# A last phase of two joined transformer blocks: the last norm and the gates move behind the join, three sums share one inverse root, the square of the polynomial goes to ScalarE

## What is computed

```python
attn = rms_norm(attn, attn_out_g) * silu(g_attn)          # 512 wide
ssm = gelu(y)                                             # 512 wide
ssm = ssm * sigmoid(ssm @ w_glu + b_glu)
ssm = rms_norm(ssm, ssm_out_g) * silu(g_ssm)
mixed = concatenate([attn, ssm]) @ w_out                  # 1024 x 1024
x = x + rms_norm(mixed, post_norm_g)
```

## Time and profile before

| | |
|---|---|
| median of 3 runs | 5829.93 us (5826.6 to 5834.68) |
| profiled execution, time | 5826.38 us |
| profiled execution, span | 5824.6 us |
| last phase, from SP's first load at 5492.85 us to the end | 332 us |
| PE busy in the whole span | 5316.9 us (91%) |
| DVE busy in the whole span | 3248.5 us (56%) |
| ACT busy in the whole span | 2129.4 us (37%) |
| mean granted clock of the tensor engine | 0.962 |

### The profile page before, as it was taken

One profiled execution on the slowest core, in us unless ns is written; L12 is line 12 of the kernel. 1 busy time (PEld: TensorE's weight loads), 2 busy tenths in 40 slices (PEclk: granted clock), 3 DMA queues, 4 the chain that ended last, 5 costly groups with the idle time before them and its releaser, 6 DMA issues. The chain is left out here.

```text
span 5824.6 us, 77622 instructions
## 1 busy us (share of the span) xinstructions
PE 5316.9 (91%) x24587; PEld 3508.7 (60%) x24922; DVE 3248.5 (56%) x6128; ACT 2129.4 (37%) x3190; POOL 707.8 (12%) x901
## 2 busy tenths in 40 slices
PE   6999999499999999999999999599995599999688
PEld 3555555366666666666666666355554477777365
DVE  3433433477676767777777777433335544443277
ACT  3111111144443545555555554222222433333243
POOL 0000000100000000000000000001003399100000
PEclk9999999699999999999999999799997799999899
DMA  3111211356464647777777676422322300000433
GB/s 136 57 50 54 72 50 50 115 176 192 159 207 150 211 152 238 237 237 240 239 232 234 229 227 204 161 93 103 103 89 97 82 5 8 6 6 6 170 108 101
DMA packets 424599, 769.80 MB, mean 132 GB/s; under 512 B 57440, under 2 KB 142368, under 8 KB 422816
## 3 DMA queue, kind: packets, MB, share of 16 engines
q1 hardware_dynamic: 363984, 607.16, 31.5%
q10 hardware_dynamic: 33216, 87.05, 4.9%
q0 software_dynamic: 27280, 74.02, 4.0%
HBM read 628.36 MB, written 139.76 MB: 132 GB/s over the span
## 5 line engine op out<-in xcount | busy, mean ns | idle before, releaser
L1070 DVE TENSOR_TENSOR w_lo<-stage,w_hi 128x1024 bf16<-128x1024 f32 (+1 forms) x800 | 929.6, 1178 | 201.3 <-ACT w_hi L939 142.3
L939 ACT ACTIVATE w_hi<-stage 128x1024 fp32r<-128x1024 f32 (+1 forms) x800 | 791.7, 1017 | 575.9 <-PE GU L773 291.2
L770 PE MATMUL GU<-w_hi,x_hl 128*128 128x512 f32 x2048 | 860.1, 420 | 19.0 <-DVE x_hl L1075 7.6
L771 PE MATMUL GU<-w_hi,x_hl 128*128 128x512 f32 x2048 | 811.6, 396 | 0.0
L636 PE MATMUL PJ<-w_in_sb,xT 128*128 128x512 f32 x1280 | 579.6, 607 | 41.9 <-ACT w_in_sb L376 31.5
L773 PE MATMUL GU<-w_lo,x_bf 128*128 128x512 bf16 x1920 | 480.6, 381 | 7.7
L770 PEld LDWEIGHTS GU<-w_hi,x_hl 128*128 128x128 f32 x2048 | 386.5, 189 | 135.1 <-issue 27.9
L770 PE MATMUL Y<-w_hi,a_hl 128*128 128x512 f32 x1024 | 456.8, 446 | 0.0
L636 PEld LDWEIGHTS PJ<-w_in_sb,xT 128*128 128x128 f32 x1280 | 244.2, 195 | 332.8 <-issue 286.2
L771 PEld LDWEIGHTS GU<-w_hi,x_hl 128*128 128x128 f32 x2048 | 387.5, 189 | 82.9
L771 PE MATMUL Y<-w_hi,a_hl 128*128 128x512 f32 x1024 | 404.4, 395 | 0.0
(11 more groups left out here) (537 smaller groups left out, 8752.2 us busy)
## 6 DMA issues: line engine op xcount, KB each, us to landing
stage<-in_expert_w_gate_up_dram SPq DMA_DIRECT2D x512, 512.0 KB, 5.2
stage<-in_expert_w_down_dram SPq DMA_DIRECT2D x224, 512.0 KB, 6.7
expert_rows<-zero_y SPq DMA_DIRECT2D x16, 2048.0 KB, 10.0
b_gu<-in_expert_b_gate_up_dram ACTq DMA_DIRECT2D x128, 256.0 KB, 4.9
expert_rows<-acted ACTq DMA_DIRECT2D x64, 512.0 KB, 2.9
b_d<-in_expert_b_down_dram ACTq DMA_DIRECT2D x32, 512.0 KB, 8.0
stage<-in_expert_w_down_dram SPq DMA_DIRECT2D x64, 256.0 KB, 3.3
z<-z_sb SPq DMA_DIRECT2D x16, 992.0 KB, 8.1
```

Of the source, the lines that this page charges most:

```text
L770: pe.matmul(out, high(k), w_high(k), start=(k == first), stop=False)
L771: pe.matmul(out, low(k), w_high(k), start=False, stop=False)
L939: act.activation(w_hi[:, c, ks, :], staged, ACT.Copy).then_inc(s["hi_done"], 1)
L1070: dve.tensor_tensor(w_lo[:, c, ks, :], staged, w_hi[:, c, ks, :], ALU.subtract).then_inc(s["lo_done"], 1)
```

## The change

- VectorE's order in body(t) becomes: g_lo(t), c_lo(t-1), pre(t), polynomial (t+1), ssm(t), gelu(t+1), join(t), `o_n` and `out` of t-2 (`add_x`), at t = 0 the low parts of the second weight, silu(t+1).
- The sum of squares of OUT goes into a third column of `ss`, and `join` makes the inverse root of tile t-2's sum in the same chain as its own two. Before the chain it also waits for `sumsq_o`. The last two tiles keep a chain of their own.
- ScalarE makes y squared (`square_y`) for t+1 ahead of tanh_p(t), after a wait for the loads of t+1. VectorE's polynomial is one operation, (y_sq + 1/GELU_A) * y, and the tanh's scale takes the factor GELU_A.
- `join` no longer waits for `silu_ready`.
- SP's and the tensor engine's instructions stay as they are.

```diff
         @block.scalar
         def _(act):
+            def square_y(t, par):
+                act.wait_ge(s["in_loaded"], t * per_in + per_in)
+                act.activation(y_sq[:, :], y_in[:, par, :], ACT.Square).then_inc(s["y_sq_ready"], 1)
+
             def ahead(t, par):
 
                 act.wait_ge(s["poly_ready"], t + 1)
-                act.activation(tanh_y[:, :], poly[:, :], ACT.Tanh, scale=GELU_S).then_inc(s["tanh_y_ready"], 1)
-                act.wait_ge(s["in_loaded"], t * per_in + per_in)
+                act.activation(tanh_y[:, :], poly[:, :], ACT.Tanh, scale=GELU_S * GELU_A).then_inc(s["tanh_y_ready"], 1)
...
+                if has_next:
+                    square_y(t + 1, 1 - par)
                 if has_this:
                     act.wait_ge(s["pre_ready"], t + 1)
                     act.activation(tanh_p[:, :], pre[:, :], ACT.Tanh, scale=0.5).then_inc(s["tanh_p_ready"], 1)
...
                 if has_prev:
                     act.wait_ge(s["o_ps"], t)
-                    if is_step(t, TILES):
-                        act.wait_ge(s["out_ready"], t - 1)
-                    act.activation(sq_o[:, :], OUT[1 - par][:, :], ACT.Square, accum_out=ss_o[:, :]).then_inc(s["sumsq_o"], 1)
-
+                    act.activation(sq_o[:, :], OUT[1 - par][:, :], ACT.Square, accum_out=ss[:, 1 - par, 2:3]).then_inc(s["sumsq_o"], 1)
+
+            square_y(0, 0)
             ahead(0, 0)
...
                 dve.wait_ge(s["in_loaded"], t * per_in + per_in)
-                y = y_in[:, par, :]
-                ch.link(dve.tensor_tensor(poly[:, :], y, y, ALU.mult))
-                ch.link(dve.tensor_scalar(poly[:, :], poly[:, :], GELU_A, 1.0, ALU.mult, ALU.add))
-                dve.tensor_tensor(poly[:, :], poly[:, :], y, ALU.mult).then_inc(s["poly_ready"], 1)
+                dve.wait_ge(s["y_sq_ready"], t + 1)
+                dve.scalar_tensor_tensor(poly[:, :], y_sq[:, :], 1.0 / GELU_A, y_in[:, par, :],
+                                         ALU.add, ALU.mult).then_inc(s["poly_ready"], 1)
...
-            def join(t, par, has_prev):
-
+            def join(t, par, has_prev, has_two):
+
+
+                n = 3 if has_two else 2
                 dve.wait_ge(s["sumsq"], t + 1)
                 dve.tensor_scalar(ss[:, par, 0:1], ss[:, par, 0:1], 1.0 / ATTN_W, EPS, ALU.mult, ALU.add)
+                if has_two:
+                    dve.wait_ge(s["sumsq_o"], t - 1)
+                    dve.tensor_scalar(ss[:, par, 2:3], ss[:, par, 2:3], 1.0 / D, EPS, ALU.mult, ALU.add)
                 ch.link(dve.tensor_scalar(ss[:, par, 1:2], ss[:, par, 1:2], 1.0 / (16 * SSM_W), EPS, ALU.mult, ALU.add))
-                rsqrt(dve, ch, rstd[:, :], ss[:, par, :], nt[:, :])
-                dve.wait_ge(s["silu_ready"], t + 1)
+                rsqrt(dve, ch, rstd[:, 0:n], ss[:, par, 0:n], nt[:, 0:n])
...
-            def last_norm(t, par, reused):
-                dve.wait_ge(s["sumsq_o"], t + 1)
-                inv_rms(dve, ch, rstd_o[:, :], ss_o[:, :], nt_o[:, :], D, EPS)
-                ch.link(dve.scalar_tensor_tensor(o_n[:, :], OUT[par][:, :], rstd_o[:, :], gain_post[:, :], ALU.mult, ALU.mult))
+            def add_x(t, par, reused):
+                ch.link(dve.scalar_tensor_tensor(o_n[:, :], OUT[par][:, :], rstd[:, 2:3], gain_post[:, :], ALU.mult, ALU.mult))
...
                 if has_prev:
                     low_cat(t - 1)
-                if has_two:
-                    last_norm(t - 2, par, reused)
                 bias(t)
-                if is_step(t, 0):
-                    low_weights()
                 if has_next:
                     gelu_in(t + 1, 1 - par)
                 unit(t)
                 if has_next:
                     gelu_out(t + 1, 1 - par)
+                join(t, par, has_prev, has_two)
+                if has_two:
+                    add_x(t - 2, par, reused)
+                if is_step(t, 0):
+                    low_weights()
+                if has_next:
                     gates(t + 1, 1 - par)
-                join(t, par, has_prev)
```

More of the change, by code:

```diff
@@ L2653, in output_phase @@
         x2 = sb("x2_6", [P, 2, D])
+        y_sq = sb("y_sq", [P, SSM_W])
         poly = sb("poly", [P, SSM_W])
@@ L2664, in output_phase @@
                             (("sq_a", ATTN_W), ("sq_s", SSM_W), ("sq_o", D)))
[L2665 to L2668, removed]
+        ss = sb("ss6", [P, 2, 3])
+        rstd = sb("rstd6", [P, 3])
+        nt = sb("nt6", [P, 3])
         cat = sb("cat", [P, 2, SSM_W])
@@ L2677, in output_phase @@
         OUT = [pb("OUT0", 2 * BANK), pb("OUT1", 2 * BANK)]
-        names = """gains glu_in out_in ident_ready w_high w_low in_loaded x_loaded poly_ready tanh_y_ready gelu_ready gT_ps g_hi_ready gT_sb gl_ps
+        names = """gains glu_in out_in ident_ready w_high w_low in_loaded x_loaded y_sq_ready poly_ready tanh_y_ready gelu_ready gT_ps g_hi_ready gT_sb gl_ps
             pre_ready tanh_p_ready ssm_ready sumsq sumsq_a tanh_g_ready silu_ready cat_ready cT_ps c_hi_ready cT_sb o_ps sumsq_o out_ready
@@ L2871, in last_norm @@
                 dve.tensor_tensor(out[:, par, :], o_n[:, :], x2[:, par, :], ALU.add).then_inc(s["out_ready"], 1)
+            def last_norm(t, par):
+                dve.wait_ge(s["sumsq_o"], t + 1)
+                inv_rms(dve, ch, rstd[:, 2:3], ss[:, par, 2:3], nt[:, 2:3], D, EPS)
+                add_x(t, par, True)
             def low_weights():
@@ L2917, in _ @@
             low_cat(TILES - 1)
-            last_norm(TILES - 2, 0, True)
-            last_norm(TILES - 1, 1, True)
+            last_norm(TILES - 2, 0)
+            last_norm(TILES - 1, 1)
         @block.tensor
```

## The result

| | before | after |
|---|---|---|
| median, 13 runs each in this comparison | 5829.93 us | 5848.16 us |
| ratio, 95% interval | | 1.0029 (1.002 to 1.0037) |
| profiled execution, span | 5824.6 us | 5846.5 us |
| first load of the last phase | 5492.85 us | 5497.35 us |
| last phase to the end of the span | 331.8 us | 349.2 us |

The kernel became slower by 18.2 us; 5851 was forecast, in a range of 5838 to 5863. What comes before the last phase took 4.5 us longer in this one execution, though the change leaves it as it was, so the phase is read from its own first load: it is 349.2 - 331.8 = 17.4 us longer.

The account below looks back on a forecast made before the run. VectorE's order was taken to bound the old kernel, and a loop through memory the new one. To `cat`(14) +19.4 us, the end +1.7: +21 us on 5829.9 gives 5851, range 5838 to 5863.

Parts of the forecast that it names:

- VectorE's order set the tile before: Last phase, old kernel: VectorE's queue takes 17.78 us a tile, and the tensor engine stands idle 2.1 us in it.
- the tensor engine's case: Rival, last phase: the tensor engine sets the tile at 16.4 us, -11 us, 5819; chance 0.05.
- The loop's length without the burst: Last phase, from `out` through SP's loads, square, join and `cat` back to `out`, transfers left out: 11.2 us.
- The burst: SP's store, x load and four loads of a later tile leaving together behind `out`: taken as 8.0 us.
- the bounds of 6.6 and 8.6: Limits for B: 6.6 us from issue and shortest landing, 8.6 us from the old kernel's two bursts end to end.
- B: Time on SP's queue from the store's issue to the last load's landing, taken as 8.0 us.
- The round: One tile of the loop through memory in the last phase: 11.2 + 8.0 = 19.2 us, 1.4 more than before.
- The start: First tiles of the last phase: low weight splits and `silu` delay GL(1) by 6.4 us; `cat`(2) at 5573.1.
- The end: Last tiles: `out`(12) and g_lo come between `cat`(14) and OUT(14), +1.7 us in the middle.
- The loop that nearly pays: Rival, last phase: with B between 5.4 and 7.2 us, the time lies within 12 us of no change; chance 0.18.
- The clock rival: Tensor engine at low clock for GL and part of OUT: its round 19.9 us, 8 us more, 5859; chance 0.07.

Follow-up runs that it names:

- experiment 1: Changed kernel with SP's body(t) storing tile t-2 and loading x of tile t, in place of t-1 and t+1: 5815.26 us, ratio 0.998 to before.
- experiment 6: Changed kernel with the last norm back in front of the bias, with its own inverse root: 5816.49 us, ratio 0.9983 to before.
- experiment 2: Kernel of experiment 1 with the second weight's split back ahead of the first polynomial: 5808.08 us, ratio 0.9966 to before.
- experiment 3: Changed kernel with only the second weight's split back ahead of the first polynomial: 5841.85 us, ratio 1.0024 to before.

## Why the prediction was right

Point by point, with what the profile after has for each:

- *VectorE's order set the tile before.* Right: with the loads out of the way (experiments 1 and 6) the tile falls to 16.36 and 16.41 us, where the tensor engine's case was worked out at 16.4.
- *The loop's length without the burst, 11.2 us.* In the tile shown, from the landing at 5664.23 to the next `out` it is 0.03 + 7.48 + 3.4 = 10.9, and 0.24 to the store's issue: 11.15.
- *The burst, 8.0 us.* From 5656.50 to 5664.23 it is 7.7, and over the 12 rounds from 7.4 to 8.35, 7.8 in the mean, within the bounds of 6.6 and 8.6. Both bounds were loose: the last load is issued 3.2 us behind the store and not 2.8, and it lands 4.5 us later and not 3.8, so the 6.6 was 1.1 too low for this tile. The upper one has 7.5 us of data, and the trace shows 6.5, with 0.7 in front of it and 0.5 behind. The 8.0 was chosen between the bounds and not worked out; that it came within 0.2 of the mean is in part luck. By the 341 GB/s that the Trainium skill gives for 1 MB (DMA: Bandwidth & Descriptors, Bandwidth) B would have been an estimated 7.3: the trace shows 322 GB/s from first to last data, 6% less, and a mean of 7.8.
- *The round, 19.2 us.* It was 18.89: 0.2 of the difference is the burst, 0.1 the rest of the loop. Over 12 rounds these 0.3 us are nearly all of the 3.7 us by which the phase stayed under the forecast's 21.
- *The start, 6.4 us lost, and its effect on `cat`(2).* GL(1) started at 5548.95 in a profile whose phase began 4.5 us late: 6.5 us later than before. `cat`(2) is 79.8 us after the phase's first load; it was 77.6 (5570.47 in the timeline), and the forecast's 5573.1 means 80.2. By the medians, experiments 1 to 3 price the late split at 6.3 and 7.2 us.
- *The end, +1.7.* From `cat`(14) to the end of the span it was 40.74 us, now 42.68: +1.9.
- Sum from the rows: +2.2 at `cat`(2), 12 x 1.11 = 13.3, +1.9: 17.4 us, which is the phase's difference.

The rivals: the tensor engine did not set the tile, since B was 7.8 and not under 5.2. The loop that nearly pays was the nearest of them: it would have begun at a B of 7.2, and B was 7.8 in the mean and 7.4 in the shortest round. The clock rival asked for 19.9 us a tile, and the mean was 18.9. But its mechanism is there, hidden as the prediction allowed: after a wait of 3.1 us the granted clock falls to about half in the middle of GL (timeline of the tensor engine, then windows with the columns of the earlier trace rows):

```profile
5619.96 0.50 PE L770 MATMUL GL<-w_hi,g_hi 128*128 128x512 f32 x1 [3.10 <-DVE g_lo L2837]
...
5620.53 0.63 PE L770 MATMUL GL<-w_hi,g_hi 128*128 128x512 f32 x1
```

```profile
5614.00:5620.00 6.00, 2.15 (x16) 1.48 (x14) 5.89 (x9) 4.37 (x7) 0.00 (x0) 1.00 0.13 53
5620.00:5624.00 4.00, 3.75 (x10) 2.46 (x12) 1.10 (x2) 0.00 (x0) 0.00 (x0) 0.57 0.96 314
```

In six of the 13 rounds of tiles 2 to 14 GL and OUT together take 15.2 to 15.4 us in place of 13.8, 1.5 more where 3.5 were feared; in experiment 1 none does. Over 5600 to 5780 us the granted clock is 0.95, against 1.00 there and 0.98 over 5560 to 5780 us in the kernel before. The chain that ended last has the load in these tiles too, and not the tensor engine, so the lost 1.5 us stayed hidden. That it costs nothing at all was only argued; no run changed the clock alone.

## What to carry to other kernels

When a store is made later, ask what is issued behind it in the same queue: here the next tile's loads, which nobody had touched, moved by the same stretch and shared one burst with it. A wait that a load ends, standing ahead of other work in an engine's queue, turns a prefetch with slack into a loop; its length is worked out by walking once round, and it sets the tile when it is longer than the round of the busiest engine. And a filler is best put where its engine waits for something else anyway: the weight split had run in such a wait and cost 6 to 7 us (medians of experiments 1 to 3) once it was moved out of it.

## What was not expected of the hardware

The mixed burst of a store, a load of x and four smaller loads moved its 2.10 MB at 322 GB/s in 6.5 us, against 298 GB/s for the store and x alone and 259 for the four loads alone: joining them saved about 1.0 us of the 7.5 that the two took apart. It stayed below the 367 GB/s of the phase's busiest stretch. Bursts of the same six transfers also differ, from 7.4 to 8.35 us between the store's issue and the last landing, and no run shows why.
